# Turning the values product of the first block's two attentions: values stationary, probabilities scaled before they are turned, results left transposed in PSUM

## The reference, cut to what matters

```python
def masked_softmax(s, mask):
    s = jnp.where(mask, s.astype(jnp.float32), NEG_INF)
    return jnp.where(mask, jax.nn.softmax(s, axis=-1), 0.0)
...
def nsa_attention(q_rot, q_raw, k_cmp, v_cmp, k_slc, v_slc, k_win, v_win, gates):
...
        o_c = jnp.einsum('grqn,ngd->qgrd', p_c.astype(v_cmp.dtype), v_cmp[b])
...
        o_s = jnp.einsum('grqk,gqkd->qgrd', p_s.astype(vs.dtype), vs)
...
        o_w = jnp.einsum('grqk,kgd->qgrd', p_w.astype(vw.dtype), vw)
...
        o = g[..., 0:1] * o_c + g[..., 1:2] * o_s + g[..., 2:3] * o_w
...
def even_mixer(h, ...):
...
    return jnp.concatenate([a_out, b_out], axis=-1) @ w_out
```

## Time and profile before

| what | us |
|---|---|
| three runs of the kernel before | 3167.7, 3168.88, 3181.07 |
| their median | 3168.88 |
| span of the profiled execution | 3175.5 |
| even mixer's attention, first score to last value product | 66.9 |
| odd mixer's attention, the same | 31.9 |

### The profile page before, as it was taken

One profiled execution on the slowest core, in us unless ns is written; L12 is line 12 of the kernel. 1 busy time (PEld: TensorE's weight loads), 2 busy tenths in 40 slices (PEclk: granted clock), 3 DMA queues, 4 the chain that ended last, 5 costly groups with the idle time before them and its releaser, 6 DMA issues. The chain is left out here.

```text
span 3175.5 us, 46878 instructions
## 1 busy us (share of the span) xinstructions
PE 3100.0 (98%) x18549; PEld 1822.6 (57%) x18549; DVE 1902.9 (60%) x3289; ACT 799.0 (25%) x2119; POOL 169.7 (5%) x157
## 2 busy tenths in 40 slices
PE   9999999999999999999999899999999999999998
PEld 7845687685468668676586576774433333333333
DVE  7743486675468644624485645532377777677776
ACT  4413443251144233223253234130200000000000
POOL 0000000000000001301000203210100000000000
PEclk9999899999999999999999999999999999999999
DMA  7542055344324541114345331033599999999993
GB/s 298 192 165 106 1 186 201 131 185 161 130 115 163 201 161 53 66 55 166 156 181 190 138 124 66 32 144 141 227 398 418 418 419 418 368 414 419 420 417 138
DMA packets 81047, 665.53 MB, mean 210 GB/s; under 512 B 10528, under 2 KB 11168, under 8 KB 14016
## 3 DMA queue, kind: packets, MB, share of 16 engines
q1 hardware_dynamic: 78816, 655.41, 52.2%
q10 hardware_dynamic: 2016, 7.13, 0.6%
HBM read 661.46 MB, written 1.05 MB: 209 GB/s over the span
## 5 line engine op out<-in xcount | busy, mean ns | idle before, releaser
L4206 PE MATMUL psum<-ring,arena 128*32 128x512 f32 x5376 | 582.2, 592 | 0.0
L4206 PEld LDWEIGHTS psum<-ring,arena 128*32 128x32 f32 x5376 | 177.5, 110 | 398.7 <-issue 397.8
L878 PE MATMUL psum<-ring,arena 128*128 128x256 f32 x1760 | 397.8, 379 | 0.0
L878 PEld LDWEIGHTS psum<-ring,arena 128*128 128x128 f32 x1760 | 334.4, 190 | 45.5
L878 PE MATMUL psum<-ring,xT_norm 128*128 128x256 f32 x1320 | 304.4, 380 | 1.3 <-DMA ring<-in_ffn_w 1.3
L931 ACT ACTIVATE arena<-arena 32x128 f32<-32x128 f32 x880 | 269.7, 306 | 31.3 <-DVE arena L1065 21.7
L990 DVE TENSOR_TENSOR ring<-ring 128x1024 f32<-128x1024 f32 x220 | 267.2, 1215 | 9.9 <-DMA ring<-in_ffn_w 3.5
L878 PEld LDWEIGHTS psum<-ring,xT_norm 128*128 128x128 f32 x1320 | 251.5, 191 | 35.9 <-DMA ring<-in_ffn_w 1.7
L4356 ACT ACTIVATE arena<-psum 128x256 f32<-128x256 f32 x84 | 32.6, 388 | 782.5 <-PE psum L4206 782.5
L898 PE MATMUL psum<-ring,arena 128*128 128x512 f32 x440 | 205.8, 592 | 0.0
L3066 PE MATMUL psum<-xT_norm,ring 128*128 128x256 f32 x832 | 184.9, 381 | 0.0
(11 more groups left out here) (634 smaller groups left out, 3946.2 us busy)
## 6 DMA issues: line engine op xcount, KB each, us to landing
ring<-in_moe_w SPq DMA_DIRECT2D x340, 1024.0 KB, 9.3
ring<-in_ffn_w SPq DMA_DIRECT2D x50, 2048.0 KB, 7.7
ring<-in_ffn_w SPq DMA_DIRECT2D x65, 1024.0 KB, 4.9
ring<-in_merge_w SPq DMA_DIRECT2D x16, 2048.0 KB, 8.6
ring<-in_feat_w SPq DMA_DIRECT2D x12, 2048.0 KB, 9.0
ring<-in_ev_in_w SPq DMA_DIRECT2D x4, 2048.0 KB, 9.0
ring<-in_od_in_w SPq DMA_DIRECT2D x4, 2048.0 KB, 9.5
ring<-in_merge_w SPq DMA_DIRECT2D x8, 1024.0 KB, 11.9
```

The costliest lines, as they stand in the source:

```text
L878: last = pe.matmul(psum[:, bank, 0:GROUP], a[:, k, :], w[:, k, :], start=(fresh and k == 0), stop=(k == KT // 2 - 1), skip_group_check=True)
L4206: last = pe.matmul(psum[part(j), r, :], xg[:, u.i, u.group // GROUPS, r * P + BLOCK * j:r * P + BLOCK * (j + 1)], m[:, j, :], start=(u.i = ...
```

## The change

- The values product has its operands swapped. Values are stationary (64 columns), the turned probabilities move (128 columns), and `x` = 0 and 1 write partitions 0 to 63 and 64 to 127 of one bank, that is, the two column halves of the array. The results come out turned: head width on partitions, queries along the free axis.
- The sums can no longer be applied afterwards, so VectorE multiplies the probabilities by gate over sum before TensorE turns them (`weigh`, one tensor_tensor over the whole group). Branches then add up in PSUM, over several groups; GpSimd's part goes.
- `turn` is two groups behind `score` and `values` three; there are three probability buffers; ScalarE copies the turned banks of group i-2 before it takes the exponentials of group i.
- Compressed groups hold 8 and 4 softmaxes in place of 6 and 6. VectorE subtracts the minimum and takes the sum, and ScalarE needs one exponential for the group.
- `score` of group i waits for the exponentials of group i-2 for all groups.
- VectorE copies finished banks to `oT` (`empty`), and `add_projection` no longer turns and copies. The 256 columns of `a_out` are turned at the start of the even attention. Rows of the even output weight are reordered on the host to fit. VectorE's row and weight sums are interleaved.
- In the odd mixer the tile `o` goes, `oT` takes its part.

```diff
+def even_rows():
+
+
+    heads = np.arange(A_WIDTH, D).reshape(2, 6, HD).transpose(1, 0, 2)
+    return np.concatenate([np.arange(A_WIDTH), heads.ravel()])
...
-            for j in range(4):
-                for i in range(2):
-                    for b in range(TB):
-                        k = 2 * j + i
-                        last = pe.transpose(prog.psum[:, 4 + j, i * S + b * P:i * S + (b + 1) * P],
-                                            sources[:, b, k * P:(k + 1) * P], prog.ident)
-                last.then_inc(turned, 1)
             for name in BLOCK_PRODUCTS:
-                first = {"P1": 0, "P2": 2}.get(name)
-                seven.on_tensor(pe, name, None if first is None else lambda k: k % 2 or pe.wait_ge(copied, first + k // 2 + 1))
+                seven.on_tensor(pe, name)
...
+            seven.mix_on_vector(dve, 0)
             seven.sum_on_vector(dve, 0)
+            seven.mix_on_vector(dve, 1)
             seven.sum_on_vector(dve, 1)
-            dve.wait_ge(copied, 4)
-            for i in range(4):
-                seven.mix_on_vector(dve, i)
+            seven.mix_on_vector(dve, 2)
             seven.sum_on_vector(dve, 2)
+            seven.mix_on_vector(dve, 3)
             seven.sum_on_vector(dve, 3)
...
+    WIDE, AWAY, BEHIND = 2 * BANK, 2, 3
+    t_sb = [mem.take(WIDE) for _ in range(3)]
...
             def score(i, g):
                 if i >= 2:
-                    if groups[i - 2].mask is None:
-                        pe.wait_ge(shifted, shifts[i - 1])
-                    else:
-                        pe.wait_ge(probs, i - 1)
+                    pe.wait_ge(probs, i - 1)
...
-                pe.wait_ge(probs, i + 1)
+                pe.wait_ge(weighted, i + 1)
...
             def values(i, g):
-                if i >= 2:
-                    pe.wait_ge(taken, outs_taken[i - 1])
+                if g.opens:
+                    before = emptied[last_use(i, g.banks)]
+                    if before:
+                        pe.wait_ge(out_copied, before)
+                    if plain and i == 0:
+                        pe.wait_ge(plain_copied, 1)
                 for x in range(2):
                     pe.wait_ge(turned_copied[x], i + 1)
-                    for j in range(g.half):
-                        m = x * g.half + j
-                        for c in range(g.blocks):
-                            at = (j * g.blocks + c) * P
-                            last = pe.matmul(psum[:, 6 + i % 2, m * HD:(m + 1) * HD], pT_sb[i % 2][0:g.keys, x, at:at + P],
-                                             g.jobs[x][j][2][c], start=(c == 0), stop=(c == g.blocks - 1))
+                opened = set()
+                for j in range(g.half):
+                    bank, to = g.places[j]
+                    for c in range(g.blocks):
+                        at = (j * g.blocks + c) * P
+                        for x in range(2):
+                            last = pe.matmul(psum[half_rows(x), bank, to:to + P], g.jobs[x][j][2][c], pT_sb[i % 2][0:g.keys, x, at:at + P],
+                                             start=g.opens and (bank, x) not in opened, stop=True, skip_group_check=True)
+                            opened.add((bank, x))
                 last.then_inc(product, 1)
 
-            for i in range(total + 2):
+            if plain:
+                for i in range(2):
+                    for b in range(TB):
+                        last = pe.transpose(psum[:, 7, i * S + b * P:i * S + (b + 1) * P], plain.source[:, b, i * P:(i + 1) * P], prog.ident)
+                last.then_inc(plain_turned, 1)
+            for i in range(total + BEHIND):
                 if i < total:
                     score(i, groups[i])
-                if 1 <= i <= total:
-                    turn(i - 1, groups[i - 1])
-                if i >= 2:
-                    values(i - 2, groups[i - 2])
+                if 0 <= i - AWAY < total:
+                    turn(i - AWAY, groups[i - AWAY])
+                if i >= BEHIND:
+                    values(i - BEHIND, groups[i - BEHIND])
...
-            def back(i, g):
-                inv = sums[:, i % 4, 0:g.count]
+                if g.mask is None:
+                    dve.wait_ge(least_ready, i + 1)
+                    dve.tensor_tensor(t, spread(least[:, i % 4, 0:g.count].unsqueeze(2), g.count, g.n), t, ALU.subtract).then_inc(centred, 1)
+
+            def weigh(i, g):
+                inv, t, n = sums[:, i % 4, 0:g.count], t_of(i, g), inverses[i]
                 dve.wait_ge(probs, i + 1)
+                if g.mask is None:
+                    dve.tensor_reduce(inv, t, AX, ALU.add).then_inc(inverse, 1)
+                    n += 1
+                    dve.wait_ge(inverse, n)
                 dve.reciprocal(inv, inv).then_inc(inverse, 1)
                 if g.gate is not None:
-                    dve.wait_ge(inverse, inverses[i] + 1)
-                    dve.tensor_tensor(g.by_branch(inv), g.by_branch(inv), g.gate, ALU.mult).then_inc(inverse, 1)
+                    dve.wait_ge(inverse, n + 1)
+                    dve.tensor_tensor(by_branch(inv, g), by_branch(inv, g), g.gate, ALU.mult).then_inc(inverse, 1)
                 dve.wait_ge(inverse, inverses[i + 1])
-                dve.wait_ge(product, i + 1)
-                if i >= 2:
-                    dve.wait_ge(added, sums_added[i - 1])
-                for branch, (out, add) in enumerate(g.outs):
-                    by = g.by_branch(inv)[:, :, branch, :]
-                    dve.tensor_tensor(product_of(i, g, tmp[i % 2], branch) if add else out,
-                                      product_of(i, g, psum[:, 6 + i % 2, :], branch),
-                                      spread(by.unsqueeze(3), *by.shape[1:], HD), ALU.mult).then_inc(taken, 1)
-
-            for i in range(total + 2):
+                dve.tensor_tensor(t, t, spread(inv.unsqueeze(2), g.count, g.n), ALU.mult).then_inc(weighted, 1)
+
+            def empty(i, g):
+                if g.out:
+                    dve.wait_ge(product, i + 1)
+                for dst, bank, n in g.out:
+                    dve.tensor_copy(dst, psum[:, bank, 0:n * P].rearrange("p (k t) -> p k t", k=n)).then_inc(out_copied, 1)
+
+            for i in range(total + BEHIND):
                 if i < total:
                     front(i, groups[i])
-                if 1 <= i <= total and groups[i - 1].count == 8:
-                    dve.wait_ge(turned, 2 * i)
-                    if i >= 3:
-                        dve.wait_ge(product, i - 2)
-                    dve.tensor_copy(pT_sb[(i - 1) % 2][:, 1, :], psum[:, 5, :]).then_inc(turned_copied[1], 1)
-                if i >= 2:
-                    back(i - 2, groups[i - 2])
-
-        @ph.block.gpsimd
-        def _(pool):
-            for i, g in enumerate(groups):
-                for branch, (out, add) in enumerate(g.outs):
-                    if add:
-                        pool.wait_ge(taken, outs_taken[i] + branch + 1)
-                        pool.tensor_tensor(out, out, product_of(i, g, tmp[i % 2], branch), ALU.add).then_inc(added, 1)
-                        pool.wait_ge(added, sums_added[i] + branch + 1)
+                if 0 <= i - AWAY < total and groups[i - AWAY].count == 8:
+                    at = i - AWAY
+                    dve.wait_ge(turned, 2 * at + 2)
+                    if at >= 2:
+                        dve.wait_ge(product, at - 1)
+                    dve.tensor_copy(pT_sb[at % 2][:, 1, :], psum[:, 5, :]).then_inc(turned_copied[1], 1)
+                if 1 <= i <= total:
+                    weigh(i - 1, groups[i - 1])
+                if i >= BEHIND:
+                    empty(i - BEHIND, groups[i - BEHIND])
...
+            def exponentials(i, g):
+                t = t_of(i, g)
+                if g.mask is None:
+                    act.wait_ge(centred, sum(h.mask is None for h in groups[:i + 1]))
+                    act.activation(t, t, ACT.Exp).then_inc(probs, 1)
+                    return
+                act.wait_ge(least_ready, i + 1)
+                if i >= 3:
+                    act.wait_ge(turned, 2 * (i - 2))
+                for m in range(g.count):
+                    x, j = m // g.half, m % g.half
+                    last = act.activation(t[:, m, :], psum[:, 2 * (i % 2) + x, j * g.n:(j + 1) * g.n], ACT.Exp,
+                                          bias=least[:, i % 4, m:m + 1], scale=-1.0, accum_out=sums[:, i % 4, m:m + 1])
+                last.then_inc(probs, 1)
...
+            if plain:
+                act.wait_ge(plain_turned, 1)
+                act.activation(plain.dst.rearrange("p i t -> p (i t)"), psum[:, 7, :], ACT.Copy).then_inc(plain_copied, 1)
...
+            for i in range(total + AWAY):
+                if 0 <= i - AWAY:
+                    copies(i - AWAY, groups[i - AWAY])
                 if i < total:
-                    g = groups[i]
-                    t = t_of(i, g)
-                    act.wait_ge(least_ready, i + 1)
```

(46 more changed lines are left out.)

62 lines of the change are left out of this document (29 added, 33 removed).

## The result

The changed kernel takes 3151.81 us (median of 4 runs, 3150.82 to 3153.51) against 3168.82 for the kernel before (4 runs, 3167.7 to 3181.07): a ratio of 0.9933, 95% interval 0.9913 to 0.9953, 17.0 us less. The forecast was 3144, between 3134 and 3158. The profiled span fell from 3175.5 to 3150.0; 3150.6 was expected.

The account below looks back on a forecast made before the run. TensorE, busy 98% of the span, was taken as the bound. Savings of 17.7 (even attention), 3.7 (odd attention) and 3.5 (projections) sum to 24.9 us; against the median of 3168.88 that gives 3144, range 3134 to 3158.

Parts of the forecast that it names:

- Parts 1 and 2: Block 1 of the even attention: values product from 1.73 to 1.06 us a group, period 3.59 us, bound by TensorE.
- Parts 3 and 4: Even attention: block 1's first mask at 319.2, not 329.96; end at 346.1 at full clock, 20.1 us less.
- the walk: Following the engines' queues step by step through the attentions to work out waits, first mask and end times.
- Part 5: Even attention: the clock doesn't hold; 7 us at 0.50 cost 2.4, leaving 17.7 us saved.
- Parts 6 and 7: Odd attention ends 3.7 us earlier; sixteen turned tiles gone from each mixer's projection save 3.5 us in all.
- the clock holds: Rival: full clock in both attentions, 28.6 us less, 3140; chance 0.15.
- falls for as long as now: Rival: the low clock still lasts 23 us, 17 us less, 3152; chance 0.12.
- Part 4: Even attention's end: 346.1 at full clock, not 366.20; 20.1 us less, about 11.5 low clock and 8.6 structure.
- halves don't overlap: Rival: column halves of the values product gain nothing, a group keeps 4.26 us; 15.5 less, 3153; chance 0.12.
- slower: Rival: clock stays low from 315 to the even attention's end and 877.8 to the odd one's; 3180; chance 0.03.

Follow-up runs that it names:

- both runs with transposes back: Changed kernel with 16 or 48 transposes, results unused, put back at the start of each projection: 3151.43 and 3164.14 us.
- the run scaled in halves: Changed kernel with VectorE scaling each group in two products of half the size, each releasing the turning of its half: 3148.38 us, ratio 0.9915 to before.
- the experiment with depth: Changed kernel with turning one group behind the scores and values two, scaling ahead kept: 3226.02 us, ratio 1.0153 to before.

## Why the prediction was right, and where it was off

| | expected saving | first profiles | new profile of before against the first of after |
|---|---|---|---|
| even attention | 17.7 | 66.90 - 49.55 = 17.35 | 58.06 - 49.55 = 8.5 |
| odd attention | 3.7 | 31.91 - 28.03 = 3.9 | 31.94 - 28.03 = 3.9 |
| projections | 3.5 | 3.4 | 3.4 |
| sum | 24.9 | 24.6 | 15.8 |

- **Parts 1 and 2** held. Values take 1.04 (1.06 expected); the border that was missed is that from turning to values, 0.09 a group, so a period is 3.66 and not 3.59. TensorE stays the bound. The Trainium skill (TensorEngine Tiling (Array Packing), Key Properties) says that a change of tiling mode drains the engine. The trace fits that in kind: the two borders cost about 0.2 (1.04 - 0.86) and 0.1 us, not the 0.38 each that the prediction had put as the worst.
- **Parts 3 and 4.** The first mask of block 1 came 22.35 us after the start where 19.9 and 2.4 of clock had been worked out, and the end after 49.55, where 49.2 had. ScalarE's pace and the waits for scaling are where the walk had them.
- **Part 5** held in size (6.8 us of low clock, 7 taken), not by its reasoning. It let the long fall end when the groups of 256 columns had come, but the first of these started at 329.96, 12 us before the clock rose. It expected falls because of the waits between 299 and 319; the clock fell at 302.7 in one profile and 303.2 in the next, in both runs with transposes back at about 315, and in the run scaled in halves not at all. The price held: 3.4 us of low clock less were 1.25 us less.
- **Parts 6 and 7** held within 0.2 us.
- **The step that failed** is the last one of the sum: it was taken from one profiled execution and then put against the median of the runs. (The rivals that the clock holds, or falls for as long as now, rest on the same fixed picture of before.) Part 4 had counted 11.5 us of the low clock as a saving. The profiled execution had 23.7 us of it in the even attention, the next one 6.8; the runs of before hold anything between. The text had noted that the span lay above two of three runs and drew nothing from it. So the mechanism was right and the forecast of 24.9 us less stands against 17.0. That the spans agree within 0.6 us is in part luck: two draws of a clock that varies went into them, and the two second profiles differ by 21.5. The structural part, 8.6 + 3.7 + 3.5 = 15.8 by the walk, was a little low: the runs less the clock show 17. In the profiles the time from the second projection's end to the span's end, where nothing was changed, is 2242.0 and 2243.1 before and 2240.2 and 2239.6 after. That can be the difference; no run explains it. With 15.8 and the range of the clock, 0 to 9, the median would have been put at 3144 to 3153.
- The rivals *halves don't overlap* and *slower* are refuted by the timeline and the runs; the experiment with depth shows what the latter one feared, a clock at 0.50 for most of both attentions, beside waits of 2 to 3 us in each group.

## What to carry to other kernels

A profile is one execution: where a stretch of it ran at the low clock, take that time out of the sum before setting it against a median of runs, or profile the same kernel twice. The same holds for an edit that seems to move or remove a fall of the clock: look first whether it does so in kernels without the edit. Work moved ahead of a step in a pipeline (here scaling ahead of turning) needs a stage of depth with it; here it decided between 17 us faster and some 50 slower than before. Outputs 64 wide in two column halves ran side by side throughout when neighbours in the queue alternated, and for about a third of a microsecond a group when they didn't.

## What the runs showed that was not expected

- The changed kernel is not only faster but steadier: 6 us between its ten runs, 19 between the first 29 of before.
- The place of the low clock varies from profile to profile with the code the same: at 302.7, 303.2 and twice about 315 in the even attention, 3.4 to 6.8 us long, and in the odd one there or not. Waits of about 1 us in work made of short matmuls lie near each of these falls, but in one profile the same first wait of 1.00 passed with none.
- 3.4 us of added TensorE work left the median where it was; in the profile the clock was low for less time elsewhere, 26.60 us for the odd attention in place of 28.03. A difference of 3 us in this kernel isn't read from medians of six runs.
